# A seventh place for expert weights in an MoE kernel, with one token tile parked in DRAM

## The reference, cut to what matters

```python
def _moe(h, w_router, router_bias, we_g, we_u, we_d, ws_g, ws_u, ws_d):
    ...                                     # top-8 of 64 experts per token -> combine (tokens x experts)
    hid = silu(einsum('td,edf->tef', t, we_g)) * einsum('td,edf->tef', t, we_u)
    routed = einsum('tef,efd->td', hid * combine[..., None], we_d)
    shared = (silu(t @ ws_g) * (t @ ws_u)) @ ws_d
    return routed + shared
...
x = x + g1 * mix                            # after the mixer
h = rmsnorm(x, norm2_g) * (1 + sc2) + sh2
x = x + g2 * _moe(h, ...)                   # g2: one row of gates for context, one for latent tokens
y = rmsnorm(x, final_norm_g)
```

## Time and profile before

| | us |
|---|---|
| three runs | 902.9, 905.97, 905.26 |
| the profiled execution, its own time | 904.02 |
| its span | 902.1 |
| PE busy in it | 875.3 |
| DVE busy in it | 478.6 |

### The profile page before, as it was taken

How to read it: one execution, slowest core, us unless ns; L and a number is a source line. 1 busy time by engine, 2 the same in 40 slices (tenths; PEclk the granted TensorE clock), 3 DMA queues, 4 the chain that set the end, 5 groups by cost and what they waited for, 6 DMA issues and landing times.

```text
span 902.1 us, 11471 instructions
## 1 busy us (share of the span) xinstructions
PE 875.3 (97%) x4211; PEld 451.5 (50%) x4211; DVE 478.6 (53%) x1047; ACT 166.6 (18%) x345; POOL 62.0 (7%) x78
## 2 busy tenths in 40 slices
PE   8999999999999999999999999999999999899994
PEld 6874446767655447644444444434444444344332
DVE  3645398936795946434344443445454544435466
ACT  4131012020000044121211212112121212112122
POOL 1020100000000000100000000000000000000001
PEclk9999999999999999999999999999999999999998
DMA  9998433421675847389999999999999999999951
GB/s 332 389 369 211 147 126 132 185 70 70 249 278 203 356 161 293 85 347 420 419 410 418 419 417 420 414 415 416 420 419 419 419 421 420 418 420 419 417 242 72
DMA packets 63194, 285.90 MB, mean 317 GB/s; under 512 B 6552, under 2 KB 6608, under 8 KB 38048
## 3 DMA queue, kind: packets, MB, share of 16 engines
q1 hardware_dynamic: 55744, 263.51, 73.6%
q0 software_dynamic: 7392, 21.63, 6.6%
HBM read 286.33 MB, written 3.80 MB: 322 GB/s over the span
## 4 chain that ended last, share of the span: by engine, by line
PE 83%; DMA 12%; DVE 2%; SPq 1%; issue 1%; ACT 1%; DVEq 0%; ACTq 0%
PE bank L1215 22%; PE bank L789 12%; DMA ring<-in_w_exp_up 10%; PE bank L1241 10%; PE bank L782 9%; PE bank L1257 7%; PE bank L1006 5%; PE bank L1053 2%; PE bank L1155 2%; DMA ring<-in_w_in 1%; PE bank L794 1%; PE bank L799 1%; PE bank L1255 1%; PE bank L961 1%; PE bank L959 1%; PE bank L1158 1%
## 5 line engine op out<-in xcount | busy, mean ns | idle before, releaser
L1215 PE MATMUL bank<-ring,QK 128*64 128x512 f32 (+1 forms) x1184 | 226.7, 595 | 5.7 <-DMA ring<-in_w_exp_up 5.5
L2215 DVE TENSOR_TENSOR hT<-bank,hT 128x512 f32<-128x512 f32 x174 | 109.7, 685 | 82.0 <-PE bank L1257 81.1
L1215 PEld LDWEIGHTS bank<-ring,QK 128*64 128x64 f32 (+1 forms) x1184 | 73.1, 129 | 143.3 <-issue 143.3
L1241 PE MATMUL bank<-ring,VG 128*64 128x512 f32 (+1 forms) x592 | 118.5, 604 | 0.0
L2204 DVE SCALAR_TENSOR_TENSOR VG<-VG,cw,bank 128x256 f32<-128x256 f32 x32 | 15.4, 480 | 171.1 <-issue 165.3
L789 PE MATMUL bank<-hT,ring 128*128 128x384 f32 x256 | 86.0, 489 | 0.0
L782 PE MATMUL bank<-ring,hT 128*128 128x512 f32 x192 | 82.7, 593 | 0.0
L1257 PE MATMUL bank<-y_hi,slotT 128*128 128x512 f32 x180 | 81.1, 451 | 1.5 <-DVE VG L2236 1.4
L1609 ACT CAST y_hi<-bank 128x512 fp32r<-128x512 f32 x64 | 34.6, 589 | 211.1 <-PE bank L1257 199.9
L1257 PE MATMUL bank<-y_lo,slotT 128*128 128x512 f32 x180 | 71.1, 395 | 0.0
L1241 PEld LDWEIGHTS bank<-ring,VG 128*64 128x64 f32 (+1 forms) x592 | 33.7, 130 | 68.0 <-issue 67.9
(11 more groups left out here) (430 smaller groups left out, 911.1 us busy)
## 6 DMA issues: line engine op xcount, KB each, us to landing
ring<-in_w_exp_gate SPq DMA_DIRECT2D x64, 1024.0 KB
ring<-in_w_exp_up SPq DMA_DIRECT2D x64, 1024.0 KB
ring<-in_w_exp_down SPq DMA_DIRECT2D x64, 1024.0 KB, 14.2
ring<-in_w_ada SPq DMA_DIRECT2D x12, 2048.0 KB, 12.0
ring<-in_w_in SPq DMA_DIRECT2D x9, 2048.0 KB, 17.9
ring<-in_w_out SPq DMA_DIRECT2D x2, 2048.0 KB, 10.3
ring<-in_w_in SPq DMA_DIRECT2D x2, 1024.0 KB, 17.1
ring<-in_w_four_out SPq DMA_DIRECT2D x4, 512.0 KB, 18.4
```

Of the source, the lines that this page charges most:

```text
L1215: ins = mm(ps[0][rows, :], xT[:, k, rows], expert(2 * s + n)[0][:, k, :, :], start=(k == 0), stop=(k == KC - 1))
L1241: ins = mm(ps[2 + h][rows, :], hidT[:, j, rows], expert(2 * s + n)[1][:, j, h * 512:(h + 1) * 512], start=(j == 0), stop=(j == 1))
L2215: v.tensor_tensor(into, o, into, ALU.add).then_inc(sem("summed"), 1)
```

## The change

The ring is cut into units of two cells. Three units make a pair: gate and up of its first expert, gate and up of its second, and both down matrices. Unit u of pair p is u = 3p, 3p+1 or 3p+2. There are six homes in the ring and a seventh, `spare`, which lies over `U` and the first tile of `x` (`x` is allocated right behind `U`). A unit takes the home of the unit seven before it; from unit 90 on (pairs 30 and 31) the home of the unit six before it among the six of the ring, so that the spare isn't used any more.

So the first unit of pair p waits for `down_done` of pair p-3, its second for `gate_up_done` of pair p-2, and its down unit also for `gate_up_done` of pair p-2 (before: two waits, both of pair p-2, the second one for `down_done`). The first unit of pair 2 goes to the spare and waits for no expert at all.

x's first tile is written to DRAM (`x0_rows`) after tile mix21 and read back behind the last weight load. The gate rows' load moves from POOL to SP, behind that. `rankT` and `slotT_next[0]` move from `U` into the table of constants. The loads for further rounds get semaphores of their own; the matmuls only read their weights at other addresses.

```diff
+PARTS = 3
+HOMES = (3, 4, 5, 2, 0, 1, 6)
+SPARE = 6
+SIX_FROM = 3 * (LAST - 2)
+def held_by(u):
+    return u - (6 if u >= SIX_FROM else 7)
+def home_of(u):
+    return HOMES[(held_by(u) if u >= SIX_FROM else u) % 7]
...
+        spare = nc.alloc_sbuf_tensor_at("spare", [P, PIECE], F32, offset=home["U"])
+        def pair_freed(eng, u):
+            p, part = divmod(held_by(u), PARTS)
+            if part == 2:
+                eng.wait_ge(sem("down_done"), 2 * (p + 1))
+            else:
+                eng.wait_ge(sem("gate_up_done"), p + 1)
...
             computed(sp, "mix21")
-            ahead(2, 2, w_ed, "down_slot0")
-            ahead(3, 0, w_eg, "gate_up_slot0")
+            for n in range(2):
+                load_down(sp, AHEAD[2 + n] * P, 1, n, "down_in1")
+            sp.wait_ge(sem("x1_ready"), 1)
+            sp.dma_start(x0_rows, x[:, 0, :]).then_inc(sem("x0_parked"), 16)
             sp.wait_ge(sem("order_ready"), 1)
             for p in range(2, PAIRS):
-                s = half_of(p)
                 e = [sp.value_load(column(tab_order, 2 * p + n), min_val=0, max_val=E - 1) for n in range(2)]
-                sp.wait_ge(sem("gate_up_done"), p - 1)
                 for n in range(2):
-                    load_gate_up(sp, e[n] * P, 2 * s + n, f"gate_up_slot{s}")
+                    if p == 2 and n == 0:
+                        sp.wait_ge(sem("x0_parked"), 16)
+                        computed(sp, "h2T01")
+                    else:
+                        pair_freed(sp, PARTS * p + n)
+                    load_gate_up(sp, e[n] * P, p, n, f"gate_up_in{p % 3}")
+                pair_freed(sp, PARTS * p + 2)
+                for n in range(2):
+                    load_down(sp, e[n] * P, p, n, f"down_in{p % 3}")
                 if p == 2:
                     computed(sp, "shT2")
                     sp.dma_start(sd_w[1], w_sd[:, 1, :]).then_inc(sem("shared_in"), 16)
-                sp.wait_ge(sem("down_done"), 2 * (p - 1))
-                for n in range(2):
-                    load_down(sp, e[n] * P, 2 * s + n, f"down_slot{s}")
+            sp.dma_start(x[:, 0, :], x0_rows).then_inc(sem("x0_back"), 16)
+            src = mod_rows[MOD_AT["g2"], :, :].rearrange("c n -> (c n)").rearrange("(o n) -> o n", o=1).broadcast_to([P, 2 * D])
+            sp.wait_ge(sem("g2_stored"), 16)
+            sp.dma_start(g2_rows.rearrange("p c n -> p (c n)"), src).then_inc(sem("g2_rows_in"), 16)
...
             computed(pool, "mix21")
-            load_rows("g2", g2_rows)
...
-            dve.wait_ge(sem("g2_rows_in"), 16)
             gate = [g2_rows[:, 0 if t == 0 else 1, :] for t in range(TT)]
...
             def residual(t):
                 if t == 0:
+                    dve.wait_ge(sem("x0_back"), 16)
+                    dve.wait_ge(sem("g2_rows_in"), 16)
                     dve.wait_ge(sem("summed"), 6 * (LAST - 2))
```

More of the change, by code:

```diff
@@ L442, in four_odd, with unit, gate_up_of, down_of @@
             return home[:, at % CHUNK:at % CHUNK + size]
[L444 to L447, removed]
+        spare = nc.alloc_sbuf_tensor_at("spare", [P, PIECE], F32, offset=home["U"])
+        def unit(u):
+            h = home_of(u)
+            return spare[:, :] if h == SPARE else ring[:, h * PIECE:(h + 1) * PIECE]
+        def gate_up_of(p, n):
+            return unit(PARTS * p + n).rearrange("p (u k f) -> p k u f", u=2, k=KC)
+        def down_of(p, n):
+            return unit(PARTS * p + 2)[:, n * CELL:(n + 1) * CELL].rearrange("p (j d) -> p j d", j=2)
         def emptied(eng, name):
@@ L476, in further_rounds, with load_gate_up @@
                     body(q)
-        def load_gate_up(sp, row, e, landed):
-            w = ring[:, e * EXPERT:(e + 1) * EXPERT]
+        def load_gate_up(sp, row, p, n, landed):
+            w = unit(PARTS * p + n)
             src = (lambda a: a[row:row + P, :]) if isinstance(row, int) else (lambda a: a[bass.ds(row, P), :])
@@ L538, in _, with load_item @@
             sp.dma_start(su_w, w_su).then_inc(sem("shared_in"), 16)
-            def load_item(n, e_slot, load, landed, count):
-                there = sp.value_load(column(tab_valid, n), min_val=0, max_val=1)
+            def load_item(item, n, load, landed, count):
+                there = sp.value_load(column(tab_valid, item), min_val=0, max_val=1)
                 with sp.If(there > 0):
-                    e = sp.value_load(column(tab_expert, n), min_val=0, max_val=E - 1)
-                    load(sp, e * P, e_slot, landed)
+                    e = sp.value_load(column(tab_expert, item), min_val=0, max_val=E - 1)
+                    load(sp, e * P, LAST - 2, n, landed)
@@ L565, in _ @@
             computed(sp, "mix20")
-            ahead(2, 0, w_eg, "gate_up_slot0")
-            ahead(2, 1, w_eu, "gate_up_slot0")
+            load_gate_up(sp, AHEAD[3] * P, 1, 1, "gate_up_in1")
             computed(sp, "mix21")
-            ahead(2, 2, w_ed, "down_slot0")
-            ahead(3, 0, w_eg, "gate_up_slot0")
+            for n in range(2):
+                load_down(sp, AHEAD[2 + n] * P, 1, n, "down_in1")
+            sp.wait_ge(sem("x1_ready"), 1)
+            sp.dma_start(x0_rows, x[:, 0, :]).then_inc(sem("x0_parked"), 16)
@@ L1240, in down @@
                         for n, rows in parts_of(p):
[L1241 removed]
+                            ins = mm(ps[2 + h][rows, :], hidT[:, j, rows], down_of(p, n)[:, j, h * 512:(h + 1) * 512],
                                      start=(j == 0), stop=(j == 1))
```

71 lines of the change are left out of this document (28 added, 43 removed).

## The result

| | before | after |
|---|---|---|
| median of 22 runs each, us | 903.54 (902.34 to 905.97) | 906.16 (905.12 to 908.24) |
| ratio | | 1.0026, 95% interval 1.0019 to 1.0033 |
| profiled execution, span, us | 902.1 | 904.9 |
| granted clock over the span | 0.994 | 0.991 |

The changed kernel is slower by 2.6 us of the medians and by 2.8 us of the two profiled spans. The prediction was 908.0 in a range of 901.0 to 912.5. Since before came out lower in 22 runs than in the first three, the difference is the better measure: +2.7 to +3.2 forecast, +2.6 measured.

What follows compares the result with a forecast made beforehand. DMA was taken to bound the last ten turns and PE those before. Lead -5.0, late gate rows +6.5 and clock +1.7 gave +3.2 us, so 907.2 or 908.5, stated as 908.0, range 901.0 to 912.5.

Steps and rivals of the forecast that it cites:

- What bounds the kernel: Expert loop: DMA sets the pace in the last ten turns, PE before; a deeper buffer gives at most 5.5 to 6.0 us.
- The prediction's sign for the lead: Profile after, last ten turns: PE waits for weights of 1 us or less would show the lead right.
- rival 2: Lead isn't realised, reload still waits at the end: 913.5 us; chance 0.16, shared with a landing later still.
- The lead: Expert loop: each load lands one unit, 5.0 us, earlier, using free DMA time before 380.85; gain 5.0, bounds 0 to 6.0.
- The parking, the moved gate load and SP's waits: Start and loop: writing out x's first tile, moving the gate load and more SP waits cost nothing, 0 us.
- The reload: End: gate rows land at 874.05, `hidden(31)` starts at 879.25, end 1.5 us later than before; a +6.5 us term.
- Its upper bound: End: tile or rows take 10.4 us behind weights at 870.3, landing at 880.7, 8.2 us late.
- The clock: End: PE idle 6.7 us, its clock falls before it restarts at 1.2 GHz; loss 1.7 us, bounds 0 and 3.5.
- The sum: Whole kernel: -5.0 for the lead, +6.5 for late gate rows, +1.7 for the clock, together +3.2 us.
- The gate rows in time: End: rows land before 872.5, so the kernel is faster, 901.8 or 900.3 us; chance 0.22.
- No dip: End: as forecast but without the dip of PE's clock, 906.8 us; chance 0.15.

Runs made afterwards that it cites:

- tenth experiment: Changed kernel with the reload of x's first tile and the gate rows issued ahead of all six loads of the last pair; 903.23 us, ratio 0.9994 to before.
- first experiment: Changed kernel without the two transfers behind the last weights and without DVE's waits for them (outputs not the layer's); 898.74 us, ratio 0.9942 to before.
- ninth experiment: Changed kernel without the two end transfers, and with pair 2's first unit also waiting for `gate_up(0)`; 901.51 us, ratio 0.9983 to before.
- third experiment: Changed kernel with the two reload transfers issued ahead of the last pair's down loads instead of behind them; 899.38 us, ratio 0.9952 to before.
- seventh: Changed kernel with reload still behind the last downs, residuals 0 and 1 moved behind `hidden(31)` in DVE's order; 899.76 us, ratio 0.9958 to before.
- second experiment: Kernel before plus only the parking and reload of x's first tile and the gate rows' load behind the last weights; 910.79 us, ratio 1.0082.
- sixth: Changed kernel with the reload ahead of the last downs and `residual(1)` moved behind `hidden(31)` in DVE's order; 899.09 us, ratio 0.9957 to before.
- 8: Changed kernel with the reload ahead of the last downs and all three residuals behind `hidden(31)`; 898.87 us, ratio 0.9945 to before.
- fifth run: Changed kernel with five extra 512-column products on PE in the gap before `hidden_T(31)`; 905.21 us, ratio 1.0017 to before.

## Why the prediction was right, step by step

**What bounds the kernel: right.** DMA sets the pace in the last ten turns. With the lead, the waits on weights shrank from 5.5 to 2.3 us in the changed kernel (0.9 to 2.8 in the other kernels with the early unit, the tenth experiment aside). The prediction's sign for the lead, 1 us or less, was not met; nor was rival 2's, 5 us again.

**The lead: right in kind, 5.0 us forecast, 4.8 measured** by the first experiment's medians. In the changed kernel's own trace it is 4.1 us at `gate_up(30)`; its start was 1.3 us later there (382.12 against 380.85), and that in the first stages of the mixer; other kernels with the same edits there started their loop anywhere from 380.6 to 382.5. The account of where the lead comes from was too narrow. It was put down to the free DMA time before 380.85; in the ninth experiment, without it, 2.1 of the 4.8 us are still there. The bigger release afterwards is the likely source, with the half clock early in the loop of before as the untested rival. So the near hit of 5.0 on 4.8, known only as 3.3 to 7.2, has luck in it.

**The parking, the moved gate load and SP's waits: nothing, right.** With the reload left out, parking and waits included, the time is 4.8 us below before, against a lead reckoned at 5.0. That bounds their cost only through that reckoning; none of these runs takes them out alone.

**The reload: right.** Landing forecast at 874.05, seen at 874.1; `hidden(31)` forecast at 879.25, seen at 879.43. Both terms of the landing held: the later of the last down loads is in 4.8 us earlier (870.5 against 875.3, 5.0 forecast), though PE was only 4.1 us earlier, and the rows 3.6 us behind it (3.75 forecast). DVE stood 4.5 us and not 6.9, since `residual(0)` was ready 2.6 us later than reckoned; that costs nothing, because the rows came last anyway. As a term, reload and clock together were put at 8.2 us; they measured 7.4 in the changed kernel and 7.3 in the kernel before. That what stands behind the wait costs is shown from both sides: moved in the queue (third experiment) or moved in DVE's order (seventh), most of it is gone. That the last parts of a transfer count is in the sixteen counts of the gate rows. They show seven of sixteen parts some 4 us and more behind the other nine, so more than the "few" of the prediction. Its upper bound took 10.4 us as the slowest broadcast; the gate rows' own load in the kernel before took 10.8, which moves nothing.

**The clock: right in kind, 1.7 us forecast.** The dip is there from 881 to 884 and takes 1.6 us in the traces; the times show 0.95 with overlapping intervals. But it didn't come as the prediction has it. There the clock has fallen before PE starts again, and PE restarts at 1.2 GHz; here PE restarted at full clock and the fall came 0.9 us later. In the second experiment, where PE stood 6.0 us, the clock did fall while it stood (0.84 in the stretch from 879 to 880, 0.50 from 880 to 884). PE's idle time was 4.4 us, not 6.7, because `gate_up(31)` began 2.4 us later than reckoned. Part of that is a second dip around 860 to 863, behind the 1.4 us wait for the duo's picks, in which the 32 down matmuls took 4.55 us instead of 3.64. The prediction didn't have it. It isn't the change's own: the second experiment, which has the old places, has it too, and the first, third and sixth experiments, which have the new ones, don't.

**The sum in the two traces.** `hidden(31)` is 1.7 us later than before (+1.5 forecast), and from there to the last down it takes 1.1 us more than before (+1.7 forecast); together that is the 2.8 us between the two spans. The clock term is less than the dip's 1.6 us because the kernel before lost some 0.5 us there too.

**The rivals.** The gate rows in time: what experiments 3, 6 and 8 came close to, at 899 us, but not this change; in the seventh they are as late as ever and it matters little, 899.8. No lead: refuted by the first experiment. No dip: the fifth run, 905.2, is what it would be, 1.6 above its before, where the prediction had 1.5.

The size of the whole was forecast as +3.2 us and is +2.6; the steps that are most off are the lead's origin and the moment at which the clock falls, and neither had much bearing on the time.

## What to carry to other kernels

A transfer at the end of a long prefetch queue lands when its last part is through behind everything ahead of it, here 25 us after its issue; before putting one there, read which engine waits for it and what stands behind that wait in the engine's own order. A deeper buffer and the price of making room for it add up separately, so test each alone: here 4.8 us gained and 7.4 lost. Either of two cheap edits of order, the reload ahead of loads that have slack or the waiting work behind work that others need, turned a loss of 2.6 us into a gain of about 4; both together gave 4.8, which isn't clear of one alone.

## What the runs showed of the hardware that wasn't expected

In float32 one product of 128 columns by 512 took two records of 0.44 us each (18 records in 7.89 us), twice the 0.22 us of the expert matmuls' records with 64 columns (32 records in 7.02 us) and four times the 0.11 us of those with 32 columns (64 records in 7.07 us). That is why nine extra products overran.

PE's granted clock fell to half for some 3 us in the last turns of some profiled executions behind a wait of only 1.4 us (changed kernel, 860 to 863; the second and eighth experiments have such a dip too) and not behind the same wait in the other nine profiles. From `gate_up(30)` to `gate_up(31)` it took 18.9 us in the changed kernel and 17.3 to 17.4 in the kernel before and the first and third experiments, so single profiles of these kernels can differ by 1.5 us in the last turns with no other cause that the traces show.

At the end of the DMA queue like transfers landed far apart: in the kernel before, of the two last down loads, issued within 1 us, one landed 16.4 us and one 23.5 us after its issue. In the changed kernel the sixteen counts of one transfer, the gate rows, came over 12.1 us. Why some parts fall behind wasn't tried.
